# The order of W and X in the triangular inverse of two scans: one half after the other, in place of both W and then both X

## The reference

```
lhs = jnp.eye(CHUNK, dtype=beta_m.dtype) + beta_m      # beta_m strictly lower triangular
u = tri_solve(lhs, bc[..., None] * vc)
w = tri_solve(lhs, (bc * jnp.exp(G))[..., None] * kc)
def step(s, inp):
    u_c, w_c, a_c, qd, kd, gl = inp
    delta = u_c - jnp.einsum('bhtk,bhvk->bhtv', w_c, s)
    o = jnp.einsum('bhtk,bhvk->bhtv', qd, s) + jnp.einsum('bhti,bhiv->bhtv', a_c, delta)
    s = gl[..., None, None] * s + jnp.einsum('bhtv,bhtk->bhvk', delta, kd)
    return s, o
```

## Time and profile before

| | |
|---|---|
| time, median of 3 runs | 4551.94 us (4547.86 to 4554.14) |
| profiled execution | 4556.42 us, its span 4554.5 us |
| mean granted TensorE clock, whole span | 0.902 |
| TensorE, matmuls (PE) | 3880.1 us, 85% of the span |
| TensorE, weight loads (PEld) | 3567.5 us, 78% |
| VectorE, ScalarE, GpSimd | 48%, 22%, 19% |
| RWKV scan | from 868 to 1446 us |
| GDN scan | from 1480 to 1785 us |

### The profile page before, as it was taken

The page is one execution under the profiler, slowest core; times in us unless marked ns, Lnnn a source line. Parts: engine busy times, 40 slices in busy tenths (PEclk is TensorE's granted clock), DMA queues, the critical chain, the costliest instruction groups (busy, mean ns, idle before and its releaser), DMA issues. The chain is left out here.

```text
span 4554.5 us, 85783 instructions
## 1 busy us (share of the span) xinstructions
PE 3880.1 (85%) x34537; PEld 3567.5 (78%) x34537; DVE 2176.3 (48%) x3749; ACT 1020.8 (22%) x1709; POOL 882.4 (19%) x712
## 2 busy tenths in 40 slices
PE   5999786577776887689999999899397789999998
PEld 4999533366665776489999998899275789999998
DVE  3333454433333554647465556400366566546555
ACT  3100244322222343422010001201154032001001
POOL 2222000000001431102222222122023212222221
PEclk7999755788898898899999999999598899999999
DMA  3222587211111222301111111222133111111111
GB/s 138 88 89 87 179 284 253 102 50 53 49 44 56 82 76 69 133 28 43 45 36 45 44 42 30 62 92 80 31 95 94 44 33 39 49 42 35 46 44 65
DMA packets 418842, 341.24 MB, mean 75 GB/s; under 512 B 62340, under 2 KB 398397, under 8 KB 416029
## 3 DMA queue, kind: packets, MB, share of 16 engines
q1 hardware_dynamic: 407137, 268.20, 19.5%
q0 software_dynamic: 10304, 60.98, 3.3%
q10 hardware_dynamic: 1152, 8.39, 0.5%
HBM read 261.01 MB, written 76.48 MB: 74 GB/s over the span
## 5 line engine op out<-in xcount | busy, mean ns | idle before, releaser
L91 POOL TENSOR_TENSOR ffn_w_lower<-ffn_w,ffn_w_upper 128x1024 fp32r<-128x1024 f32 x164 | 393.3, 2398 | 1358.4 <-DVE ffn_w_upper L86 1358.4
L938 DVE SCALAR_TENSOR_TENSOR rstd<-u_tile,ffn_taps,rstd 128x945 f32<-128x945 f32 (+3 forms) x440 | 489.8, 1113 | 86.0 <-ACT rstd L885 72.0
L99 PE MATMUL ffn_ps<-HU,ffn_w_upper 128*128 128x384 f32 x2112 | 481.4, 335 | 28.7 <-DVE ffn_w_lower L91 25.7
L99 PE MATMUL ffn_ps<-HL,ffn_w_upper 128*128 128x384 f32 x2112 | 480.7, 335 | 0.0
L99 PE MATMUL ffn_ps<-HU,ffn_w_lower 128*128 128x384 f32 x2112 | 480.3, 335 | 0.0
L99 PEld LDWEIGHTS ffn_ps<-HU,ffn_w_upper 128*128 128x128 f32 x2112 | 376.8, 188 | 31.5 <-issue 28.8
L99 PEld LDWEIGHTS ffn_ps<-HL,ffn_w_upper 128*128 128x128 f32 x2112 | 377.5, 188 | 0.0
L99 PEld LDWEIGHTS ffn_ps<-HU,ffn_w_lower 128*128 128x128 f32 x2112 | 377.3, 188 | 0.0
L99 PE MATMUL ffn_out_ps<-g_upper,ffn_w_upper 128*128 128x384 f32 x1056 | 355.4, 337 | 22.9 <-DVE g_lower L91 14.4
L99 PE MATMUL ffn_out_ps<-g_lower,ffn_w_upper 128*128 128x384 f32 x1056 | 354.2, 335 | 0.0
L99 PE MATMUL ffn_out_ps<-g_upper,ffn_w_lower 128*128 128x384 f32 x1056 | 354.1, 335 | 0.0
(11 more groups left out here) (461 smaller groups left out, 6313.6 us busy)
## 6 DMA issues: line engine op xcount, KB each, us to landing
ffn_w<-in_ffn_w_in_dram SPq DMA_DIRECT2D x88, 512.0 KB
ada_w<-in_ada_w_dram SPq DMA_DIRECT2D x40, 1024.0 KB, 5.4
rwkv_units<-unit_rows POOLq DMA_DIRECT2D x8, 2304.0 KB, 8.6
un<-rwkv_units SPq DMA_DIRECT2D x36, 512.0 KB, 3.7
z_even<-z_tile POOLq DMA_DIRECT2D x31, 576.0 KB, 3.1
in_w<-in_ab_w_in_dram SPq DMA_DIRECT2D x31, 512.0 KB
gun<-gdn_units SPq DMA_DIRECT2D x72, 192.0 KB, 3.7
z_odd<-z_tile POOLq DMA_DIRECT2D x24, 576.0 KB, 4.9
```

Of the source, the lines that this page charges most:

```text
L91: return eng.tensor_tensor(out.bitcast(F32R), x, up, ALU.subtract)
L99: mm = pe.matmul(o, w(a).bitcast(F32R), r.bitcast(F32R), start=(first and n == 0), stop=(last and n == 2))
L938: dve.scalar_tensor_tensor(out=o, in0=i, scalar=tp[:, t:t + 1], in1=o, op0=ALU.mult, op1=ALU.add).then_inc(s["conv"] if n < NCONV else s[" ...
```

## The change

From level 2 on, TensorE issues W and X of the first half and then W and X of the second, where it issued W of both and then X of both. Level 1 stays, and so does RWKV's last level. The list of names in `block_order` follows. VectorE's and ScalarE's code is the same.

```diff
@@ block_order
+        elif kind == "pe" and l > 1:
+            out += [f"{q}{n}{l - (n == 'x')}" for q in prs for n in ("w", "x")] + [f"{q}dy{l}" for q in prs]
         elif kind == "pe":
             out += [f"{q}{n}{l - (n == 'x')}" for n in ("w", "x", "dy") for q in prs] if l else [f"{q}y0" for q in prs]
@@ rwkv_scan_phase, slot
                         for l in range(1, NL - 1):
-                            each(block_w, l)
                             if l == 1:
+                                each(block_w, l)
 
                                 ac.wait(pe, f"{a}v1", it)
-                            each(block_x, l)
+                                each(block_x, l)
+                            else:
+                                for g in range(2):
+                                    block_w(pe, ps, st, K, B, a + g, g, l)
+                                    block_x(pe, ps, st, K, B, a + g, g, l)
                             beside(l, 0)
                             each(block_dy, l)
                             beside(l, 1)
@@ gdn_scan_phase, slot, level
                                 st = steps_of(new)
-                                for part in (block_w, block_x, block_dy):
-                                    if part is block_dy and old is not None and l <= 4:
-
-                                        (out if l <= 2 else update)(old, (l - 1) % 2)
+                                for parts in ((block_w,), (block_x,)) if l == 1 else ((block_w, block_x),):
                                     for g in range(2):
-                                        part(pe, ps, st, K, B, new[1] + g, g, l)
+                                        for part in parts:
+                                            part(pe, ps, st, K, B, new[1] + g, g, l)
+                                if old is not None and l <= 4:
+
+                                    (out if l <= 2 else update)(old, (l - 1) % 2)
+                                for g in range(2):
+                                    block_dy(pe, ps, st, K, B, new[1] + g, g, l)
```

## The result

The changed kernel takes 4528.26 us (median of 7 runs, 4522.14 to 4534.28), the kernel before 4550.43 us (7 runs, 4537.28 to 4554.14): a ratio of 0.9955, 95% interval 0.9942 to 0.9968.

What follows compares the result with a forecast made beforehand. TensorE's own work was taken to bound the RWKV scan; RWKV +12 us (14.6 less 1 and 1.5) and GDN 0 on 4556.4 gave 4568.4, less 4.5 for the median: 4564 us, +0.26%, range 4549 to 4580.

Steps and rivals of the forecast that it cites:

- The price of the order: RWKV level at full clock: W, X, W, X takes 1.50 us against 1.21, +0.29 us for two more tile changes.
- GDN in sum: GDN scan: levels 2 to 4 lose 5 us, levels 5, 6 and the first slot gain; sum 0, between -5 and +6.
- the 1.5 us taken for it: GDN level 6: ScalarE's X copies start 0.3 us sooner in half of the slots, -1.5 us.
- The shorter wait of W for Y: TensorE's wait for VectorE's Y at W, 5.5 us in RWKV and 11.3 in GDN, should shrink in both scans.
- the end of the wait for `S_scaled`: RWKV level 4: the next run's wait for GpSimd, 2.3 us in 7 slots, should shrink, covering the 0.29 us.
- the slots' terms: RWKV levels 2 to 5: 0.29 + 0.19 + 0.12 + 0.21 = 0.81 us a slot, 14.6 us in 18 slots.
- the last term of RWKV's sum: RWKV scan: 1.5 us taken off for added time falling just ahead of an "issue" wait, which it shortens.
- The instruction supply: Rival: time added between instruction arrivals comes off the next "issue" wait; RWKV 0 to +4, 4552 to 4556 us; chance 0.15.
- My argument against it: RWKV level 2's run at 1129.01 to 1130.22 has no "issue" wait, and many levels between two waits would still pay.
- The halves' rival: First half's X reaches ScalarE 0.3 us sooner, so dY, Y and next W come sooner; 4544 us with free seams; chance 0.10.
- The full price: Rival: no wait covers the seams, 72 x 0.29 = 21 us in RWKV and GDN +5; +26, 4578 us; chance 0.15.
- The clock: Rival: more TensorE pauses lower the granted clock, one more half-clock level per RWKV slot, 14 us: 4578 us; chance 0.10.

Runs made afterwards that it cites:

- gdn_only: New order at levels 2 to 6 of the GDN scan alone, RWKV in the old order, against the kernel before: 4539.92 us, 1.0006.
- rwkv_only: New order at levels 2 to 5 of the RWKV scan alone, GDN in the old order, against the kernel before: 4527.36 us against 4539.61, 0.9982.
- the shift of 128: 128 semaphore increments on TensorE ahead of the RWKV slots and 128 behind, in both orders, against the kernel before: old order 1.0037, new order 1.0029.
- after_again: The changed kernel measured once more, word for word, against the kernel before: 4539.64 us against 4552.65, 0.9974.
- split_w1: RWKV levels 2 to 5 with half of the second half's W ahead of the first X, GDN as before, against the kernel before: 4525.15 us against 4543.01, 0.9956.
- before_small_load: Old order, RWKV loads of `un` bring 16 of 128 partitions from the third step on (stale data), against the kernel before: 4532.13 us, 0.9973.
- before: The kernel before the change, old order in both scans, nothing added: 4550.43 us in the first comparison.
- before_shift128: Old order with 128 semaphore increments on TensorE ahead of the RWKV slots and 128 behind, against the kernel before: 4554.93 us, 1.0037.

## Why the prediction was wrong

**Right.** The price of the order: 1.53 us for W, X, W, X against 1.50 forecast, and 1.21 before. GDN in sum: 0 forecast, 1.0006 (0.9994 to 1.0018) measured in `gdn_only`, with level 5's dY at 1.52 us against 1.50. GDN's wait of dY at level 6 for ScalarE did not shrink, though (4.7 us in 9, 5.0 in 10 after), so the 1.5 us taken for it were not seen. The shorter wait of W for Y and the end of the wait for `S_scaled`: both seen. RWKV's TensorE does more: 9 us more busy time in the scan in the first pair and 13.7 from `gdn_only` to `rwkv_only`, where the granted clock is alike; the slots' terms gave 14.6.

**The step that failed** is the last term of RWKV's sum, "1.5 us for added time that falls just ahead of an 'issue' wait and shortens it". I took absorption for an exception and sized it so. In this scan it is the rule: every 256 instructions, some 5 us, TensorE stands at "issue", so every seam lies ahead of such a wait. Against the 1.5 us of that term, the waits fell by 27 us in the first pair of profiles, by 17 to 24 with 64 to 192 increments and by 14 from `gdn_only` to `rwkv_only`; the busy time that was added is 9, 14 to 20, and 14 us. In these pairs all of it was absorbed, with 0.5 to 18 us beyond. Not in every pair: it was 22 of 24 us with the shift of 128, and 10 of 19 from `gdn_only` to `after_again`, on different chips. The earlier trace rows held two of the lines; I did not sum the others, which make 106.4 us in all.

**The rivals.** The instruction supply was the right mechanism, and I set its floor too high, at 0 to +4: I had the wait give back what is added, and nothing beyond. My argument against it, that level 2's run has no such wait in it, looked too near: the wait stands in the very next run, 1.10 us (1131.88). The halves' rival, the only one I gave a faster time, is refuted as a cause: `split_w1` holds the first X back and is as fast. The full price was not paid. The clock explains neither direction. Time at half clock in the RWKV scan went from 143 to 113 us in the first pair by the trace's clock records, but the old order has 108 us in `gdn_only` and the new one 114 in `after_again`; with 64 and 128 increments it rose (134 to 158, 124 to 134), and with 192 it stayed at 108. At the one place shown the clock fell behind the longer wait: after 2.63 us of standing still the next block ran at 0.53, after 1.77 at 1.00. In other passes of the changed kernel it was 0.54 and 0.64 after waits of 1.70 us.

The Trainium skill, Runtime: NRT & Kernel Launch, section Instruction fetch mechanics, has instructions come in blocks of 16 KiB, 256 of them, and calls the cost of crossing one mostly hidden. The trace agrees with the first: the DMA view of the changed kernel from 1100 to 1132 us has six such packets,

```profile
q8 instruction: 6, 0.10, 1.3%
```

0.10 MB in six, and the waits lie 256 instructions apart. It disagrees with the second: 71 to 111 us of a scan of 558 to 603 are "issue". The same section of the Trainium skill says that a taken branch breaks the prefetch; the rows of L1762, where the loop starts anew, agree: of their 20.9 us in 8 waits, six waits stand at the loop's start, 3.1 to 3.6 us each.

**Open.** Why the fetch starts sooner in the new order. In the third stretch the next block came 5.47 us after the one before it, where it had been 6.42, although TensorE was busier; 0.61 us of the difference is the packet's earlier start (2.84 us after the block's start instead of 3.45), the rest its shorter time and landing. The load of `un` is excluded as the reason there. What asks for a fetch, and so what an order has to bring forward, no run here tests. Nor is it settled why no level gives the gain alone, and how much of the 22 us is this place's: 22 and 13 us in two comparisons at this place, 8 in the mean of the four.

## What to carry to other kernels

Where the "issue" waits of the engine that sets the pace return every 256 instructions, sum them over all lines before pricing an edit: here work added between two of them was taken off the next, and the price that the timeline showed at full clock was more than the cost. This kernel's time also depended on where its blocks end, by 0.88% between 64 and 192 increments at the start; so compare two orders at several places, and try a few places as a change of its own. One profile of the scan varies by some 14 us for the same code, so a cause read from a single pair needs the medians behind it.

## What the runs showed of the hardware

- TensorE waited at the end of most blocks of 256 instructions in a stretch of small matmuls, mostly 0.5 to 2.7 us and up to 3.5, up to 3.8 at the loop's start, and 4.1 to 4.7 behind the loop in the shifted kernels, though the blocks shown at full clock held only 3.4 to 4.6 us of work.
- Each such wait of over 0.5 us (1046 in 20 profiles) ended 1.0 to 2.0 us after a 16 KiB packet of instructions had landed. A load that kept the DMA engines busy moved the start of the packet from 2.67 to 4.06 us after the block's start at one place (`before_small_load`, `before`).
- A change of tile from 64x64 to 128x128 and back cost 0.15 and 0.20 us, an estimate from the earlier trace rows; two more changes a level gave the 0.32 us seen (1.53 - 1.21).
- Semaphore increments on TensorE, one after the other, started 0.15 us apart (1447.12, 1447.27, 1447.42 us in `before_shift128`); 128 of them lengthened the stretch behind the scan by 15 us (11.9 to 26.8).
- The place of the block ends, moved by 64 to 192 increments at the start, was worth from +0.30% to -0.58% in the old order.
